# The attention heads of a hybrid diffusion step in another order: keys, transposed values and queries of the next head behind the scores, squares summed on four column groups

## The reference

```python
q = rms_norm((cq @ w_uq).reshape(B, T, N_HEADS, QK_DIM), q_hn)      # QK_DIM = 128 + 64
kvu = (ckv @ w_ukv).reshape(B, T, N_HEADS, QK_NOPE + V_DIM)
k_nope, v = kvu[..., :QK_NOPE], kvu[..., QK_NOPE:]
k = rms_norm(jnp.concatenate([k_nope, k_pe], axis=-1), k_hn)
s = jnp.einsum('bqhd,bkhd->bhqk', qblk, k).astype(jnp.float32) * scale
p = jax.nn.softmax(s, axis=-1).astype(v.dtype)
return jnp.einsum('bhqk,bkhd->bqhd', p, v)
```

## Time and profile before

| | us |
|---|---|
| median of 3 runs | 1814.4 |
| the profiled execution | 1802.15 |
| its span | 1800.2 |
| TensorE busy in it | 1714.7 |
| the eight heads (start of the first scores to start of the output product) | 307.5 |

### The profile page before, as it was taken

How to read it: one execution, slowest core, us unless ns; L and a number is a source line. 1 busy time by engine, 2 the same in 40 slices (tenths; PEclk the granted TensorE clock), 3 DMA queues, 4 the chain that set the end, 5 groups by cost and what they waited for, 6 DMA issues and landing times.

```text
span 1800.2 us, 27041 instructions
## 1 busy us (share of the span) xinstructions
PE 1714.7 (95%) x11526; PEld 1661.6 (92%) x11526; DVE 967.0 (54%) x1673; ACT 630.1 (35%) x1015; POOL 241.9 (13%) x288
## 2 busy tenths in 40 slices
PE   4888999999999999999999999999999999999998
PEld 2877888889999999999999999998999999999998
DVE  3655455454667654455535889997773223223232
ACT  1433333333545342243324652454542221222111
POOL 1000001100003553344334200001000000000000
PEclk9987989999999999999999999998999999999999
DMA  7211221101323453444333301110022222222211
GB/s 304 68 50 45 67 70 62 68 25 41 111 73 117 147 158 115 127 146 139 119 111 118 98 26 47 48 48 24 25 71 94 71 71 82 83 71 71 71 63 67
DMA packets 127872, 153.47 MB, mean 85 GB/s; under 512 B 11553, under 2 KB 114921, under 8 KB 126728
## 3 DMA queue, kind: packets, MB, share of 16 engines
q1 hardware_dynamic: 113128, 98.77, 17.5%
q0 software_dynamic: 13952, 50.34, 8.5%
q10 hardware_dynamic: 672, 2.62, 0.4%
HBM read 148.93 MB, written 2.79 MB: 84 GB/s over the span
## 4 chain that ended last, share of the span: by engine, by line
PE 78%; DVE 14%; ACT 3%; issue 2%; POOL 1%; DMA 1%; SPq 0%; DVEq 0%; ACTq 0%; POOLq 0%
PE PS L591 24%; PE PS L593 22%; PE PS L596 22%; DVE YACC L1901 7%; ACT WH L1074 1%; DVE WL L1422 1%; PE PS L685 1%; PE PS L658 1%; PE PS L814 1%; DVE PTL L1759 1%; PE PS L804 1%; PE PS L801 1%; DMA ROWS<-in_mla_k_hnorm 1%; PE PS L838 1%; PE PS L800 1%
## 5 line engine op out<-in xcount | busy, mean ns | idle before, releaser
L591 PE MATMUL PS<-HH,WH 128*128 128x320 f32 x1776 | 411.1, 313 | 14.3 <-DVE HL L1551 6.2
L593 PE MATMUL PS<-HL,WH 128*128 128x320 f32 x1776 | 405.9, 310 | 0.0
L596 PE MATMUL PS<-HH,WL 128*128 128x320 f32 x1776 | 404.3, 309 | 0.0
L1422 DVE TENSOR_TENSOR WL<-RAW,WH 128x2048 fp32r<-128x2048 f32 (+1 forms) x96 | 216.9, 2259 | 204.2 <-ACT WH L1074 203.6
L591 PEld LDWEIGHTS PS<-HH,WH 128*128 128x128 f32 x1776 | 296.9, 189 | 16.9 <-issue 5.2
L593 PEld LDWEIGHTS PS<-HL,WH 128*128 128x128 f32 x1776 | 299.4, 189 | 0.0
L596 PEld LDWEIGHTS PS<-HH,WL 128*128 128x128 f32 x1776 | 298.9, 189 | 0.0
L1074 ACT ACTIVATE WH<-RAW 128x2048 fp32r<-128x2048 f32 (+1 forms) x96 | 173.7, 1809 | 112.3 <-PE PS L596 112.3
L1563 DVE SCALAR_TENSOR_TENSOR X<-PS,MODV,X 128x128 f32<-128x128 f32 (+2 forms) x192 | 72.4, 433 | 206.6 <-PE PS L596 206.5
L591 PE MATMUL PS<-HIDH,WH 128*128 128x320 f32 x704 | 162.3, 312 | 1.0 <-DVE HIDL L1838 0.7
L568 POOL TENSOR_TENSOR BGACC<-BGACC,BGW 128x512 f32<-128x512 f32 x98 | 134.9, 1377 | 200.3 <-ACT BGW L1268 199.2
(11 more groups left out here) (280 smaller groups left out, 2467.0 us busy)
## 6 DMA issues: line engine op xcount, KB each, us to landing
BGW<-in_w_mod POOLq DMA_DIRECT2D x112, 256.0 KB, 3.0
RAW<-in_ffn_w_gate SPq DMA_DIRECT2D x22, 1024.0 KB, 5.3
RAW<-in_ffn_w_up SPq DMA_DIRECT2D x22, 1024.0 KB, 5.3
RAW<-in_ffn_w_down SPq DMA_DIRECT2D x16, 1024.0 KB, 4.9
MODA<-in_w_mod POOLq DMA_DIRECT2D x48, 256.0 KB, 3.7
RAW<-in_conv_w_pw SPq DMA_DIRECT2D x16, 512.0 KB, 5.1
RAW<-in_ffn_w_down SPq DMA_DIRECT2D x8, 768.0 KB, 4.2
MODS_A<-in_w_mod POOLq DMA_DIRECT2D x5, 1024.0 KB, 15.6
```

What stands on the lines that cost most here:

```text
L591: mm(o, wh, xh, start=first, stop=False)
L593: mm(o, wh, xl, start=False, stop=False)
L596: ins = mm(o, wl, xh, start=False, stop=last)
L1422: V.tensor_tensor(WL[:, u % 2, 0:n], RAW[:, u % 2, 0:n], WH[:, u % 2, 0:n].bitcast(F32), ALU.subtract).then_inc(lo_done, 1)
```

## The change

It does five things in the attention of layer 0.

- **Order.** The unit of head h+1 is used for the keys first, then the values, then the queries, directly behind the scores of head h. The split of unit h+2 moves in front of `keys(h+1)` on ScalarE and VectorE. The rotation and its high part go into functions of their own, `rotate_queries` and `rotary_high`, further back.
- **Values.** They are made transposed, channels on partitions (`values_across`, tile `vt`: 12 products of 384 columns, as for the keys), copied to `VT` by ScalarE, and turned back by 6 transposes (`values`).
- **Squares.** `head_sums` (tile `hsum`) has 32 columns of ones as the stationary operand and lets the squares move, 384 columns at a time: two groups for the queries (tiles 0 to 2 and 2 to 4), two for the keys, each with its own 32 output partitions. ScalarE copies the four groups (`HROW`), and 3 transposes (`head_stat`, tile `hst`) turn them between the second and the third weighted sum. `head_norm` reads one number for each group and tile; `RQ` is written behind the diagonals.
- **Modulation.** The two halves of a row go to two tiles, the second behind the values; VectorE adds them (`add_rows`), and the row is turned behind the key spread.
- **Copies.** Tiles with 128-column pieces lie without a gap over their two banks (`flat`), so that one instruction reads them where two did (`PTH`, `PTL`, `RK`).

The diff, cut to what matters:

```diff
+            def head_sums(h):
 
...
+                ps = begin(("hsum", h))
                 pe.wait_ge(sem("qn_hi"), h + 1)
                 pe.wait_ge(sem("pe_sq"), h // 2 + 1)
-                for t in range(QT):
-                    o = ps[:, 0, t:t + 1]
-                    mm(o, QSQ[:, t * P:(t + 1) * P], ONES[:, 0:1], start=True, stop=False)
-                    mm(o, PESQ[lo:hi, t * P:(t + 1) * P], ONES[lo:hi, 0:1], start=False, stop=True)
                 pe.wait_ge(sem("kn_hi"), h + 1)
-                for t in range(NKT):
-                    ins = mm(ps[:, 0, QT + t:QT + t + 1], KSQ[:, t * P:(t + 1) * P], ONES[:, 0:1], start=True, stop=True)
+                out = [ps[COLG * g:COLG * (g + 1), 0, 0:3 * P] for g in range(GROUPS)]
+                q = (slice(0, 3 * P), slice(2 * P, TOK))
+                for g in range(2):
+                    mm(out[g], ONES[:, 0:COLG], QSQ[:, q[g]], start=True, stop=False)
+                for g in range(2):
+                    mm(out[2 + g], ONES[:, 0:COLG], KSQ[:, 3 * P * g:3 * P * (g + 1)], start=True, stop=True)
+                for g in range(2):
+                    ins = mm(out[g], ONES[lo:hi, 0:COLG], PESQ[lo:hi, q[g]], start=False, stop=True)
...
+            def head_stat(h):
+
+                ps = begin(("hst", h))
+                was_read(pe, ("hsum", h))
+                for i in range(3):
+                    ins = tr(ps[:, 0, i * P:(i + 1) * P], HROW[:, i * P:(i + 1) * P], EYE[:])
+                ins.then_inc(mm_done, 1)
...
+            def modulate(j, step):
+                ps = begin(("ma", j, step))
...
-                ins.then_inc(mm_done if step else sem("rows_used"), 1)
+                             start=True, stop=True)
+                ins.then_inc(mm_done, 1)
 
...
+            def values_across(h):
+                s = U[("head", h)] % 2
+                product(("vt", h), (WH[:, s, :], WL[:, s, :]), 512 + P, KVT, 256, CKH, CKL, n=KEYS // 2).then_inc(mm_done, 1)
+
             def values(h):
-                s = U[("head", h)] % 2
                 ps = begin(("v", h))
+                was_read(pe, ("vt", h))
                 for t in range(NKT):
-                    o = ps[:, t // 3, (t % 3) * P:(t % 3 + 1) * P]
-                    for k in range(KVT):
-                        wa = 512 + k * 256 + P
-                        ks = slice(t * P, (t + 1) * P)
-                        mm(o, CKH[:, k, ks], WH[:, s, wa:wa + P], start=(k == 0), stop=False)
...
                 if more:
+                    keys(h + 1)
+                    values_across(h + 1)
                     queries(h + 1)
-                for t in range(QT):
+                for t in range(3):
+                    turn(h, t)
+                if more:
+                    head_sums(h + 1)
+                for t in range(3, QT):
                     turn(h, t)
                 if more:
                     rotate_queries(h + 1)
                     if h < N_ROWS:
-                        rows = begin(("ma", h))
-                        modulate(rows, h, 0)
-                    keys(h + 1)
+                        modulate(h, 0)
+                was_read(pe, ("v", h))
+                weighted(h, 0)
+                weighted(h, 1)
+                if more:
                     head_stat(h + 1)
-                    if h < N_ROWS:
-                        modulate(rows, h, 1)
-                was_read(pe, ("v", h))
-                for g in range(3):
-                    weighted(h, g)
-                if h < N_ROWS:
-                    turn_rows(h)
+                weighted(h, 2)
                 if more:
                     values(h + 1)
+                    if h < N_ROWS:
+                        modulate(h, 1)
                     key_spread(h + 1)
+                    if h < N_ROWS:
+                        turn_rows(h)
...
+
+            def add_rows(h):
+                n = ("ma", h, 1)
+                filled(dve, n)
+                was_read(dve, ("ma", h, 0))
+                V.tensor_tensor(MROWA[:], MROWA[:], tile2(n)[:, 0, :], ALU.add).then_inc(free_of(n), 1)
...
                 if h + 1 < HEADS:
+                    split_units(U[("head", min(h + 2, HEADS - 1))])
+                    keys(h + 1)
                     queries(h + 1)
...
                 if h + 1 < HEADS:
-                    keys(h + 1)
+                    rotate_queries(h + 1)
                     head_norm(h + 1)
                     rotary_low(h + 1)
+                    values(h + 1)
                 if h < N_ROWS:
+                    add_rows(h)
                     mod_read_chunk(("mb", h), 2 + h // 2, 4 * (h % 2), 4)
-                if h + 1 < HEADS:
-                    values(h + 1)
```

The tables of `tile_order` and `LAST` follow the same order; two of their lines:

```diff
+            o += [("kn", h + 1), ("vt", h + 1), ("qn", h + 1), *even(h + 1, "pe")]
+            o += [("v", h + 1), *mb, ("rk", h + 1), *mt]
```

More of the change, by code:

```diff
@@ L273, in program @@
         KSQ = sb("KSQ", [P, KEYS], R_T[0])
+        HROW = sb("HROW", [P, 3 * P], R_T[0])
+        VT = sb("VT", [P, KEYS], R_T[6])
         QNH = sb("QNH", [P, TOK], R_T[4], F32R)
@@ L780, in keys @@
             def keys(h):
+                if h:
+                    unit_begin(("head", h))
                 s = U[("head", h)] % 2
@@ L892, in _ @@
             rotate_queries(0)
+            values_across(0)
+            head_sums(0)
             head_stat(0)
@@ L1170, in queries @@
             def queries(h):
-                round_units(U[("head", min(h + 1, HEADS - 1))])
                 n = ("qn", h)
@@ L1185, in keys, with values_across, sum_rows, rotary_high @@
                 filled(act, n)
-                k2 = lambda r: r.rearrange("p (b t) -> p b t", b=2)
-                A(k2(KSQ[:]), tile2(n)[:, :, 0:KEYS // 2], ACT.Square)
-                A(k2(KNH[:]), tile2(n)[:, :, 0:KEYS // 2], ACT.Copy).then_inc(sem("kn_hi"), 1)
+                A(keys2(KSQ[:]), tile2(n)[:, :, 0:KEYS // 2], ACT.Square)
+                A(keys2(KNH[:]), tile2(n)[:, :, 0:KEYS // 2], ACT.Copy).then_inc(sem("kn_hi"), 1)
+            def values_across(h):
+                n = ("vt", h)
+                filled(act, n)
+                A(keys2(VT[:]), tile2(n)[:, :, 0:KEYS // 2], ACT.Copy).then_inc(free_of(n), 1)
+            def sum_rows(h):
+                n = ("hsum", h)
+                filled(act, n)
+                A(HROW[:], tile2(n)[:, 0, 0:3 * P], ACT.Copy).then_inc(free_of(n), 1)
+            def rotary_high(h):
                 if h % 2 == 0:
@@ L1201, in round_output @@
                 A(OH[:, k, :], O[:, k, :], ACT.Copy).then_inc(sem("o_hi"), 1)
+            round_units(U[("head", 1)])
             queries(0)
@@ L1242, in _ @@
                 if h < N_ROWS:
-                    filled(act, ("ma", h))
-                    A(MROWA[:], tile2(("ma", h))[:, 0, :], ACT.Copy).then_inc(free_of(("ma", h)), 1)
+                    filled(act, ("ma", h, 0))
+                    A(MROWA[:], tile2(("ma", h, 0))[:, 0, :], ACT.Copy).then_inc(free_of(("ma", h, 0)), 1)
                 for g in range(3):
@@ L1249, in _ @@
                     A(O[:, h, a:b], tile2(n)[:, 0, 0:b - a], ACT.Copy).then_inc(free_of(n), 1)
+                    if g == 1 and h + 1 < HEADS:
+                        rotary_high(h + 1)
                 if h + 1 < HEADS:
@@ L1633, in queries @@
             def queries(h):
-                split_units(U[("head", min(h + 1, HEADS - 1))])
                 n = ("qn", h)
@@ L1687, in split_output @@
                 V.tensor_tensor(OL[:, k, :], O[:, k, :], OH[:, k, :].bitcast(F32), ALU.subtract).then_inc(sem("o_split"), 1)
+            split_units(U[("head", 1)])
             queries(0)
```

126 lines of the change are left out of this document (67 added, 59 removed).

## The result

The changed kernel takes 1765.45 us (median of 4 runs, three of them within 1761.43 and 1765.6), the kernel before, run beside it, 1813.79 us. The ratio is 0.9726, 95% interval 0.9707 to 0.9745. One run of the changed kernel (1869.4 us, at a lower granted clock) is left out of this, and is not explained.

The account below looks back on a forecast made before the run. TensorE, with 78% of the chain, was taken as the bound. Seven heads gave 43.7 us and the setup 4.0, less 5 for low stretches: 43 off 1814.4, so 1771 us, range 1756 to 1793.

Parts of the forecast that it names:

- Squares: Sums of squares in each head: 5.86 us replaced by 1.5 for six matmuls and 0.4 for transposes, gain 4.0.
- The rule of the Trainium skill on one-column matmuls: Sums of squares: by it the 32 old matmuls take under 1 us, and the change loses about 1 a head.
- Values: Values of each head: 4.06 us replaced by 2.19 for products and 0.79 for transposes, gain 1.1 us.
- Waits: TensorE's waits in a head: 2.48 us go, two new ones come; net 0.3 for odd heads, -0.5 for even.
- The wait of 1.0 and 1.8 us in front of the turned row: New wait of TensorE for VectorE's chain from the filled `hst`: 1.0 us for odd heads, 1.8 for even.
- Clock: Second modulation half and weighted sums: clock stays up without one-column matmuls, 1.8 us a head; 5 us off for remaining stretches.
- The 8.7 us that the prediction held against that rule: Stretch before the sums, with 21 transposes and 2.4 us without work, where the clock stayed at 1.00.
- the prediction's own sign of being wrong: In the heads: a stretch at 0.50 of over 7 us a head would show the forecast wrong.
- Setup: In front of the heads: steps shorter by 5.5 us at the low clock, scores lose 1.5, gain 4.0 us.
- another sign of being wrong: A wait of over 2 us for the diagonals would show the forecast wrong.
- The step from profile to median: Whole kernel: the runs' median lies 12.2 us above the profiled one, so 1759 profiled becomes 1771 for the median.
- The rival of a clock that stays low from the waits into the scores: Heads: 1.2 GHz from the wait before `hsum` through the next scores and beyond; slower, up to 1940 us; chance 0.02.

Follow-up runs that it names:

- e5: The changed kernel with the 36 value products and the one-column sums put back, only the new order kept: 1827.6 us, 1.0082 of the kernel before.
- e9: The changed kernel with the 36 value products put back, the order and the sums on four column groups kept: 1778.15 us, 0.9803 of the kernel before.
- e2: The kernel before with only the squares summed on four column groups and turned, in the old order: 1794.78 us, 0.9927 of the kernel before.
- e6: The changed kernel with the turned row's narrow products repeated eight times more in heads 0 to 5: 1877.38 us, 1.0374 of the kernel before.
- e7: The kernel of e6 with the rotary scores over all 128 rows, which computes another output: 1821.08 us, 1.0050 of the kernel before.
- e11: The kernel of e6 with every score product over rows 0 to 63, which computes another output: 1869.43 us, 1.0300 of the kernel before.
- e3: The changed kernel with the turned modulation row moved behind the keys of the next head but one: 1757.86 us, 0.9718 of the kernel before.
- e1: The kernel before with only the values made transposed, in the old order: 1784.86 us, 0.9878 of the kernel before.
- e8: The changed kernel with e3's turned row and rotary scores over all rows, the other head's queries zeroed: 1740.65 us, 0.9605 of the kernel before.
- e4: The changed kernel with the rotary part of the scores over all 128 rows, which computes another output: 1738.47 us, 0.9611 of the kernel before.

## Why the prediction was right

The forecast of 1771 us was 5.5 us high; range and sign held. The steps for the sums and for the waits came out nearly as laid out. That the total came so close is in part luck, as the last two steps below show. By its steps:

- **Squares** (4.0 us a head). Right in size: 1.55 us for the sums and 0.25 to 0.35 for the transposes, where 1.5 and 0.4 stood. The four column groups run side by side: four products of 384 columns take 0.78 us (167.27 to 168.05), as long as the two of `PESQ` behind them (0.77). Against the sums at the full clock (4.5 us in `e5`) the gain is 2.6 us; the rest of the 4.0 is clock, which the forecast had not parted from it.
- **The rule of the Trainium skill on one-column matmuls** (TensorEngine Tiling (Array Packing), section Instruction Overhead: one column costs as much as about 60) was rightly set aside. The trace disagrees with it: 32 recorded matmuls take 4.5 us at the full clock, 0.14 each. The 12 of the keys, all on 128 rows, take 0.11 each (`e5`, 234.95 to 236.31), the 20 that go back and forth between `QSQ` on 128 and `PESQ` on 64 rows 0.16 (231.84 to 234.95).
- **Values** (1.1 us a head). The new steps measure 2.1 (159.12 to 161.20) and 0.74 us, as set, but little of the gain reached the end: 0.6 us or nothing in the heads with a modulation row. The sentence that a late landing of `MODA` would fall in the wait for the turned row named the place; that it would eat another step's gain was not in the sum. `e9` shows it, and shows what the sum had at nothing: the values were worth 11 us by the clock of the setup and head 0.
- **Waits.** The one for `QNL` was exact (1.20; 0.5 for even heads against 0.4). VectorE's chain from the filled `hst` to `MROWA` was 5.6 us for 5.9 forecast. The wait of 1.0 and 1.8 us in front of the turned row was mis-sized: 0.6 us, twice, which fits TensorE coming 1 us later from the modulation row.
- **Clock** (1.8 us a head, and 5 us taken off for three stretches of 1.7). That the one-column matmuls bring the falls held: `e5` to `e9` is 49 us, and `e2` has no fall left in heads 1 to 6. The rule of the Trainium skill in TensorE: Matmul & The Clock Gate, Part 4, that transposes don't count as work for the clock, brought no fall here: with nine more of them a head the clock was at 1.00 in heads 1, 3, 5 and 6. The 8.7 us that the prediction held against that rule were a weaker witness than it says, as 3.6 of them are query products. The price of the stretches that remain failed: two, not three, but each cost 7 us instead of 1.7, 14 us in all. The 1.7 left out that a stretch of 6.8 us costs 3.4 us of work wherever it lies; before, half of it lay under the sums. And it was taken from products on full rows, while these two run over scores on half rows, which `e6`, `e7` and `e11` show to stay low for longer. They are also the prediction's own sign of being wrong, a stretch at 0.50 of over 7 us a head, and it came in two of seven heads.
- **Setup** (4.0 us). It brought 7.4 us from the first keys product to the first scores. The forecast priced its steps at the low clock, but it was back at 1.00 from 137.8 to 144.7 us, and the scores lost 0.65 us to it, where 1.5 stood. Another 2.75 us came ahead of the first keys product, where two low stretches of before are 6.8 us long and those of the changed kernel 3.4. That is not the change's: both lengths turn up there among the kernels below (6.8 us at 110 us in `e3` and `e5`, 3.4 in `e1`, `e8` and `e9`). The wait for the diagonals is in the 7.4 us (2.5 us at 144.45); over 2 us for them was another sign of being wrong, and it came here, though not in the heads (0.7).
- **The sum.** In the profiles the gain is 36.5 us where 43 stood: 29.7 in the heads against 38.7, 10.2 in front of them against 4, and 3.0 given back behind.
- **The step from profile to median** (1771 is 12 us above the 1759 forecast for the profile) then failed the other way: the changed kernel's median is that of its profile. The profile came out 6.5 us above its forecast, and the 12 us did not come; that these two misses met is luck.

The rival of a clock that stays low from the waits into the scores, which I gave 0.02, comes nearest to heads 2 and 4, and to `e5` as a whole, where the new order costs 15 us. It had the wrong cause. The waits don't hold the clock down: `e5` waits 7.4 us less than before and has the lower clock. In `e6` and `e11` a narrow stretch lowers it and the half-row scores don't bring it back. In heads 2 and 4 of the changed kernel the fall itself comes about 2 us into the scores, and both taking the turned row away (`e3`) and filling the rows (`e4`) did away with it; which of the two does how much is not shown, and neither is why heads 1, 3 and 5, with the same steps in front of their scores, keep the clock.

## What to carry to other kernels

Look at what runs behind a place where TensorE does little. Score products of 320 columns on full rows brought the clock back in 3.5 to 6.8 us; half-row ones often did not before they ended, and neither did 36 products of 128 columns on full rows in 10 us. So the same quiet microsecond has very different prices. Give matmuls on 64 rows zeros in the other rows, if the zeros are cheap: it saves the changes of rows and the clock. Parts of a change that share a clock, or a late transfer, don't add up: time them in the order in which they will stand.

## What the runs showed that I had not expected

- Once the granted clock had fallen ahead of the scores, it stayed at 0.50 for 17 to 22 us behind the first score, the whole of 14 or 17 us of gapless score products and a few microseconds of keys, when half or all of the score products used 64 rows, and for 3.5 to 6.8 us when all used 128. Why half rows fail to raise it stays open: the trace shows the granted clock, not what it is taken from.
- 36 gapless value products on 128 rows, of 128 columns each, and the key spread behind them ran for 10.2 us at 0.50 in three kernels, without a rise.
- Reordering alone cost 15 us with less waiting (7.4 us less for `PTL`). The clock went with it: 0.82 in the heads against 0.92.
- A change between 64 and 128 rows costs 0.19 us of TensorE in the scores, 14 us over eight heads.
